# The gate and up steps of a decoder layer: who forms the weight-block sums of the third joint product

## The reference

```python
def conv_ffn(h, prev, w_gate, w_up, cw, cb, w_down):
    g = h @ w_gate
    ext = jnp.concatenate([prev, g], axis=1)
    a = jax.nn.silu(causal_dwconv(ext, cw, cb)) * (h @ w_up)
    return a @ w_down, ext[:, ext.shape[1] - (FFN_CONV_W - 1):]
```

## Time and profile before

| | before |
|---|---|
| median of 3 runs | 3131.33 us (3131.06 to 3133.97) |
| profiled execution | 3129.62 us, of which the span of the trace is 3128.0 us |
| PE busy | 3035.2 us, 97% of the span |
| DVE busy | 1853.2 us, 59% |
| ACT busy | 367.8 us, 12% |
| POOL busy | 181.9 us, 6% |
| gate and up steps 1 to 21 | from 1489.09 us of the span on, 48.79 us each where nothing is late |

### The profile page before, as it was taken

How to read it: one execution, slowest core, us unless ns; L and a number is a source line. 1 busy time by engine, 2 the same in 40 slices (tenths; PEclk the granted TensorE clock), 3 DMA queues, 4 the chain that set the end, 5 groups by cost and what they waited for, 6 DMA issues and landing times.

```text
span 3128.0 us, 43789 instructions
## 1 busy us (share of the span) xinstructions
PE 3035.2 (97%) x15994; PEld 2517.4 (80%) x15994; DVE 1853.2 (59%) x3616; ACT 367.8 (12%) x910; POOL 181.9 (6%) x232
## 2 busy tenths in 40 slices
PE   8999999899888999999999999999999999999998
PEld 7888887788556886777889988899888878888786
DVE  6899252354557434448666767767676675345434
ACT  3000020111443002031000000000000000000112
POOL 0000000100012000002000000000000032021011
PEclk9999999999999999999999999999999999999999
DMA  7222223341218323734232322323223244233322
GB/s 238 68 67 67 84 88 116 107 133 31 81 45 305 113 80 119 241 101 152 82 114 81 108 98 85 114 81 108 101 83 114 87 144 140 82 121 86 89 72 80
DMA packets 301370, 336.93 MB, mean 108 GB/s; under 512 B 12568, under 2 KB 280476, under 8 KB 298575
## 3 DMA queue, kind: packets, MB, share of 16 engines
q1 hardware_dynamic: 295498, 309.43, 30.7%
q0 software_dynamic: 5760, 26.03, 2.5%
HBM read 306.41 MB, written 38.18 MB: 110 GB/s over the span
## 4 chain that ended last, share of the span: by engine, by line
PE 76%; DVE 3%; ACT 1%; DMA 1%; issue 1%; DVEq 0%; SPq 0%; ACTq 0%
PE ps L1066 26%; PE ps L1883 19%; PE ps L1877 12%; PE ps L1422 6%; PE ps L1037 3%; PE ps L1814 2%; PE ps L1659 2%; PE ps L1313 2%; PE ps L1461 1%; ACT xT_region_b L2160 1%; PE ps L1560 0%; PE ps L1449 0%; DMA weight_ring<-in_w_ffn_up 0%; PE ps L1450 0%; PE ps L1505 0%
## 5 line engine op out<-in xcount | busy, mean ns | idle before, releaser
L1883 PE MATMUL ps<-region_f 128*128 128x272 f32 x1344 | 319.2, 393 | 0.0
L1883 PEld LDWEIGHTS ps<-region_f 128*128 128x128 f32 x1344 | 254.5, 191 | 51.3
L1042 PE MATMUL ps<-xT_region_b,weight_ring 128*128 128x272 f32 x1216 | 279.9, 393 | 1.6 <-ACT region_f L1974 1.0
L1042 PEld LDWEIGHTS ps<-xT_region_b,weight_ring 128*128 128x128 f32 x1216 | 230.8, 190 | 49.5 <-issue 2.2
L1066 PE MATMUL ps<-region_c,weight_ring 128*128 128x272 f32 x768 | 184.2, 392 | 1.4 <-DVE region_c L3380 1.4
L2556 DVE SCALAR_TENSOR_TENSOR rstd_and_scratch<-ext,tile_taps,rstd_and_scratch 128x512 f32<-128x512 f32 x240 | 180.5, 752 | 8.5
L1066 PE MATMUL ps<-xT_region_b,weight_ring 128*128 128x272 f32 x736 | 174.5, 392 | 1.1 <-DVE weight_ring L2440 1.1
L1066 PEld LDWEIGHTS ps<-region_c,weight_ring 128*128 128x128 f32 x768 | 145.8, 190 | 31.7 <-DVE region_c L3376 1.8
L1066 PEld LDWEIGHTS ps<-xT_region_b,weight_ring 128*128 128x128 f32 x736 | 139.5, 190 | 30.1 <-issue 1.5
L1883 PE MATMUL ps<-xT_region_b,weight_ring 128*128 128x272 f32 x672 | 160.9, 392 | 0.0
L1883 PE MATMUL ps<-xT_region_b,v_tok 128*128 128x272 f32 x672 | 160.9, 392 | 0.0
(11 more groups left out here) (483 smaller groups left out, 4825.6 us busy)
## 6 DMA issues: line engine op xcount, KB each, us to landing
weight_ring<-in_w_ffn_gate SPq DMA_DIRECT2D x44, 1024.0 KB, 4.9
weight_ring<-in_w_ffn_up SPq DMA_DIRECT2D x44, 1024.0 KB, 7.1
weight_ring<-in_w_in SPq DMA_DIRECT2D x36, 1024.0 KB, 5.2
weight_ring<-in_w_ffn_down SPq DMA_DIRECT2D x32, 896.0 KB, 5.8
weight_ring<-in_w_out SPq DMA_DIRECT2D x16, 1024.0 KB, 5.1
gated_spill<-region_c SPq DMA_DIRECT2D x19, 544.0 KB, 2.7
weight_ring<-in_w_ffn_down SPq DMA_DIRECT2D x16, 640.0 KB, 4.7
residual_spill<-xT_region_b SPq DMA_DIRECT2D x2, 4352.0 KB, 18.3
```

The costliest lines, as they stand in the source:

```text
L1042: mm = pe.matmul(PS[:, 2 * j + h, 0:HALF], lhs(kt), rhs(kt, h), start=(kt == 0), stop=(kt == n - 1))
L1883: mm = pe.matmul(PS[:, B_BANK[k][r], 0:HALF], lhs[:, t, :], rhs[:, t, :], start=(t == 0), stop=(t == 7))
```

## The change

GpSimd forms the four weight-block sums of joint product 6. DVE's call is taken out, POOL gets the same four operations in two loops over the 21 steps, and the counts move from `s_dsum` (12 in a step, now 8) to `s_hd` (4 in a step), on which PE then waits in joint product 6. The operations, their tiles and the point from which they may start (the slabs loaded, joint product 0 done) are the same. POOL runs them between its token-block sums and those of the down projection.

```diff
         def deep_sum_at(i, base, r, n):
-            return i * 12 + (DSUM0 + 12 * (base - 1) + {0: 0, 1: 4, 6: 8}[r] + n)
+            return i * 8 + (DSUM0 + 8 * (base - 1) + 4 * r + n)
+
+        def sixth_sum_at(i, base, n):
+            return i * 4 + (HD0 + 12 + 4 * (base - 1) + n)
...
                     if m in (2, 3, 5):
-                        pe.wait_ge(s_dsum, deep_sum_at(i, base, r, {2: 2, 3: 3, 5: 4}[m]))
+                        n_ = {2: 2, 3: 3, 5: 4}[m]
+                        if r == 6:
+                            pe.wait_ge(s_hd, sixth_sum_at(i, base, n_))
+                        else:
+                            pe.wait_ge(s_dsum, deep_sum_at(i, base, r, n_))
...
                 deep_blocks(0, 0, s_quad)
-                deep_sums(i, base, 6, at_body(i, base, 2))
                 deep_blocks(1, 3, s_quad)
...
+            def sixth_sums(i, base=0):
+                j, half, _ = DEEP[6]
+                w, v = ffn_w(0, 8), ffn_w(1, 8)
+                a11, a12, a21, a22 = w[:, j, 0:4, half, :], w[:, j, 4:8, half, :], v[:, j, 0:4, half, :], v[:, j, 4:8, half, :]
+                s1, s2, s3, s4 = WDEEP[6]
+                for k in range(2):
+                    pool.wait_ge(s_fw[k][j], i * 16 + 16 * (GU // 2 + base + 1))
+                pool.wait_ge(s_prod, at_body(i, base, 2))
+                pool.tensor_tensor(s1, a21, a22, ALU.add).then_inc(s_hd, 1)
+                pool.wait_ge(s_hd, sixth_sum_at(i, base, 1))
+                pool.tensor_tensor(s2, s1, a11, ALU.subtract).then_inc(s_hd, 1)
+                pool.tensor_tensor(s3, a11, a21, ALU.subtract).then_inc(s_hd, 1)
+                pool.wait_ge(s_hd, sixth_sum_at(i, base, 2))
+                pool.tensor_tensor(s4, a12, s2, ALU.subtract).then_inc(s_hd, 1)
+
+            with pool.Fori(1, STEPS_GU - KEPT) as i:
+                sixth_sums(i)
+            with pool.Fori(0, KEPT) as i:
+                sixth_sums(i, STEPS_GU - KEPT)
```

## The result

| | before | changed |
|---|---|---|
| median | 3131.33 us (5 runs, 3129.39 to 3133.97) | 3148.16 us (5 runs, 3144.72 to 3150.84) |
| ratio to before | 1 | 1.0055, 95% interval 1.0044 to 1.0066 |
| profiled execution | 3129.62 us | 3144.72 us |
| span of its trace | 3128.0 us | 3142.7 us |

The change costs 17 us (14 to 21). The profiled execution of the changed kernel is the fastest of its five, and lies 15.1 us above the profiled one of before. POOL's new sums are L3529, L3531, L3532 and L3534. The recorded expectations name L3318 by its line before the change.

A forecast was written before the change was run, and what follows sets the result against it. PE, busy 97% of the span, was taken as the bound. Costs of 4.2 + 4.2 + 3.15 + 2.6 + 1.0 + 1.8 + 0.9 = 17.9 us on 3131.3 gave 3149 us, range 3137 to 3162 (8 in 10).

The forecast's parts named there:

- What is removed is worth nothing: Four DVE sums after L3318, 2.8 us a step, lie off the critical path; gain 0, at most 6.6 us.
- A POOL sum of 128x512 takes 1.25 us, a collision 1.05 us: A POOL sum queued ahead of a DVE operation with both inputs in SBUF delays DVE by 1.05 us.
- POOL is ready 0.3 us after joint product 0: In each step POOL's sums may start about 0.3 us after joint product 0, for the semaphore.
- Fifteen ordinary steps have one collision inside their margin: In steps like step 12 only L3298 is caught: 1.05 us against at least 1.5 us of margin, cost 0.
- Steps 2, 8 and 9 pay 3.6 us: Two collisions exceed the smaller margins at L3318: 1.3 us each in steps 8 and 9, 1.0 in step 2.
- Step 1 is 58.3 us, step 20 is 56.6 us: Four collisions, 4.2 us, without margin in each; step 20 also loses 1.8 us to the slow clock.
- Step 21 waits 3.3 us and has an even chance of the slow clock: Three collisions, 3.15 us, without margin in step 21, plus 0.9 us as half of a 1.8 us clock loss.
- PE doesn't wait for POOL: In joint product 6 PE needs POOL's second sum about 13 us after POOL's fourth ends, so the wait costs nothing.
- The rival in which steady steps have two collisions each: Fifteen ordinary steps have two collisions, 2.1 us against margins of 1.5 to 2.0: +6 us, 3155; chance 15%.
- The rival in which DVE keeps the way: DVE's sums L3292 to L3298 run without letting POOL in, so the change is hidden: price 0, 3131 us; chance 13%.
- The rival with two collisions in each late step: Only steps 1, 20 and 21 pay, with two collisions each: 6 to 10 us, 3139; chance 9%.

The follow-up runs named there:

- the kernel without the sums: Changed kernel with the four sums of joint product 6 left out on both engines and PE's new waits gone: 3129.88 us, ratio 0.9995 to the kernel before.
- the one with both: Kernel before with all DVE sums kept, plus the same four sums on POOL into an unread tile, PE waiting for POOL's fourth: 3148.61 us, ratio 1.0053.
- the kernel with the 18 early steps: Changed kernel with POOL starting at joint product 0 in steps 2 to 19, but behind L3318 in steps 1, 20 and 21: 3135.09 us, ratio 1.0014.
- the split with POOL early: Changed kernel with deep_blocks(0) moved between the second and third sum of block_sums(0), POOL still starting at joint product 0: 3133.49 us, ratio 1.0008.
- the kernel with the three early steps: Changed kernel with POOL starting at joint product 0 in steps 1, 20 and 21 only, behind L3318 in steps 2 to 19: 3147.28 us, ratio 1.0046.

## Why the prediction was right

3149 was forecast, 3148.16 measured, 17.9 us of cost against 17, and the mechanism is the one forecast. That the number is so close is in part luck, since terms were off both ways. By its steps:

- **What is removed is worth nothing.** Right, shown by the kernel without the sums and by the one with both.
- **A POOL sum of 128x512 takes 1.25 us, a collision 1.05 us.** Measured 1.27 alone and 2.29 - 1.22 = 1.07.
- **POOL is ready 0.3 us after joint product 0.** Measured 0.25 us.
- **Fifteen ordinary steps have one collision inside their margin.** Right. L3305 is at 2.29 us in steps 2 to 19, L3299, L3301 and L3302 are at 1.22 or 1.23, and each of these steps takes 48.79 or 48.80 us.
- **Steps 2, 8 and 9 pay 3.6 us.** Wrong in this execution: none pays. I had taken the late slabs of one execution as a property of the steps. Their lateness is a matter of the run, and the kernel with the 18 early steps shows what it costs when it comes: 1.5 us in each of three other steps. Over its eleven runs that kernel costs 4 us (2 to 7), about the 3.6 of the term, though only one of them has a trace, so how much of the 4 us is late slabs is not shown. PE waits for L3325 in three steps and not in five or six, 15.6 us and not 20.
- **Step 1 is 58.3 us, step 20 is 56.6 us.** Measured 58.18 and 56.88. Step 1 is right term by term. Step 20 is right by luck: a slab landed 1.0 us later there, and the collisions cost less than 4.2. Before, DVE waited 2.93 us for the slab and began 2.7 us ahead of the step; in the changed kernel it waited 3.94 us and began 1.7 us ahead. The row of before, then that of the changed kernel:

```profile
2418.74 0.69 DVE L3223 TENSOR_TENSOR xT_region_b<-weight_ring 128x512 f32<-128x512 f32 x1 [2.93 <-DMA weight_ring<-in_w_ffn_up]
```

```profile
2422.53 0.69 DVE L3230 TENSOR_TENSOR xT_region_b<-weight_ring 128x512 f32<-128x512 f32 x1 [3.94 <-DMA weight_ring<-in_w_ffn_up]
```

 Two of the four collisions are with small sums of the kept step, ahead of L3299, and not with L3302 and L3305:

```profile
2430.93 1.41 POOL L3529 TENSOR_TENSOR xT_region_b<-weight_ring 128x512 f32<-128x512 f32 x1 [42.63 <-PE ps L1884]
2431.14 1.51 DVE L3397 TENSOR_TENSOR region_c<-region_c  x1
2432.42 1.36 POOL L3531 TENSOR_TENSOR xT_region_b<-xT_region_b,weight_ring 128x512 f32<-128x512 f32 x1
2432.79 1.29 DVE L3399 TENSOR_TENSOR region_c<-region_c  x1
...
2434.00 2.29 DVE L3299 TENSOR_TENSOR region_f<-weight_ring 128x1024 f32<-128x1024 f32 x1
2435.17 2.24 POOL L3534 TENSOR_TENSOR xT_region_b<-weight_ring,xT_region_b 128x512 f32<-128x512 f32 x1
2436.32 2.17 DVE L3301 TENSOR_TENSOR region_f<-region_f,weight_ring 128x1024 f32<-128x1024 f32 x1
```

 L3397 and L3399 take 0.44 us alone, so a small sum waits 1.07 and 0.85 us, about as long as a large one. The `cmp_w` product comes 18.42 us after the step's start and came after 13.78. Of these 4.6 us 1.0 is the slab and 3.6 are the collisions. In the kernel with both engines, where the slab of step 20 is only 0.2 us later than before, it comes after 17.81 us, so four collisions cost 3.8 us there.
- **Step 21 waits 3.3 us and has an even chance of the slow clock.** It waited 3.2 us and got the slow clock, 0.59 over 3.4 us. The term was 4.9 us (3.2 and 1.7) where I had 3.15 + 0.9.
- **PE doesn't wait for POOL.** Right.

The terms that came out otherwise are -3.6 in steps 2, 8 and 9 and +0.9 in step 21. With these the sum is 15.2 us, and the profiled executions are 15.1 us apart, closer than it deserves, with 1.0 us of late slab inside step 20 and 1.35 us gained ahead of the steps. The rival in which steady steps have two collisions each is out by the row of step 12, and L3302 is at 1.22 us in all of steps 2 to 19. The rival in which DVE keeps the way is out by every timeline shown: neither engine gets a second exposed instruction in while the other waits. The rival with two collisions in each late step is out too: steps 1 and 20 have four and step 21 has three.

One reading was too narrow. I counted only DVE operations with both inputs in SBUF as exposed, but the copy L3202 in the earlier trace rows has one input, in SBUF, and it waits as well: 1.30 us beside POOL, against a median of 0.175 us over its 44 executions in that trace. It changes no count here, since no such copy lies ahead of L3318.

The Trainium skill ("SBUF — State Buffer", section "Who interferes with whom") says that a VectorE instruction with two SBUF inputs contends with a GpSimd instruction that reads SBUF, and one with at most one doesn't, outside the modes in which VectorE uses two ports. The runs agree on both halves, with L3305 at 2.29 us and L3325 at 0.44 us beside POOL sums. Whether the copy L3202 ran in such a mode no run shows. The skill's "GPSIMD Engine Reference" (section "3.1 Elementwise — side-by-side cycle accounting") gives 4497 ns for 2048 columns. An estimate from it in proportion is 1.12 us for 512, and 1.27 was measured. By that estimate the prediction's sum would be about 2 us smaller and not 1, since its terms count 17 collisions and each would be 0.13 us cheaper. 256 columns take 0.73 us here, so doubling the columns adds 0.54 us, and about 0.2 us of a call doesn't grow with them.

## What to carry to other kernels

Before work is moved from VectorE to GpSimd, ask from what moment it may start and which exposed VectorE operations (two SBUF inputs, and here a copy within SBUF too) lie between that moment and the next one that TensorE waits for. Each such meeting cost VectorE nearly the whole GpSimd instruction, 1.07 of 1.27 us, more than the 0.69 us of VectorE time that the moved operation set free. The same work costs 17 us or nothing depending on one wait. And a busy share (59%) says nothing on a late engine: what counts is the margin at the one operation that another engine needs, step by step, and putting that operation ahead of work with slack gained 7 us where moving work gained none.

## What the runs showed of the hardware

- A wait of TensorE costs more than its length once the clock falls. After 3.2 us of wait (step 21) the granted clock was 0.59 over 3.4 us, mostly at 1.2 GHz, and 1.7 us were lost. After 6.2 us (step 20) it was 0.50. After the 1.6 us of step 20 of before it stayed at 2.4 GHz. The length of the wait doesn't set the price. From the start of the `cmp_w` product to the end of the step an ordinary step takes 36.75 us. It took 1.8 us more in step 1 of before (wait 3.2), 1.6 and 1.7 more in steps 1 and 20 of the changed kernel (waits of 6.2), but 2.6 more in step 1 of the split with POOL early (wait 3.9) and 3.1 more in step 1 of the kernel with the three early steps (wait 6.2). What decides between these is not shown.
- When both engines have exposed work queued, they change places after each instruction. In the eleven meetings of steps 1, 20 and 21 of the changed kernel no engine had two in a row while the other waited.
- A meeting costs VectorE the GpSimd instruction less 0.2 us: 1.07 us at 512 columns, 0.53 at 256.
